# First loads in order of use, one weight block converted earlier, and the first pairs' squared ReLU on another engine

## The reference

```python
h = rmsnorm(x, norm_mix[0]); z = h @ w_in                       # 1024 -> 2304
xa, gc, gb, q, k, v = split(z)
ya = gb * conv3(gc * xa)                                        # causal, width 3
yb = windowed_attention(rmsnorm(q), rmsnorm(k), v, sinks)       # window 128
x = x + concat([ya, yb]) @ w_out
x = x + square(relu(rmsnorm(x, norm_mlp[0]) @ w_up[0])) @ w_down[0]     # 1024 -> 4096 -> 1024
h = rmsnorm(x, norm_mix[1]); x = x + pool_mix(h) * scale        # trailing means of 2, 4, 8, 16
x = x + square(relu(rmsnorm(x, norm_mlp[1]) @ w_up[1])) @ w_down[1]
```

## Time and profile before

| | |
|---|---|
| median of 3 runs | 1857.74 us (1857.17 to 1860.59) |
| the profiled execution | 1856.85 us |
| its span | 1855.1 us |
| PE busy, of the span | 1794.6 us (97%) |
| DVE, ACT, POOL busy | 1286.3, 698.8, 97.2 us |

### The profile page before, as it was taken

How to read it: one execution, slowest core, us unless ns; L and a number is a source line. 1 busy time by engine, 2 the same in 40 slices (tenths; PEclk the granted TensorE clock), 3 DMA queues, 4 the chain that set the end, 5 groups by cost and what they waited for, 6 DMA issues and landing times.

```text
span 1855.1 us, 33339 instructions
## 1 busy us (share of the span) xinstructions
PE 1794.6 (97%) x13805; PEld 1752.4 (94%) x13805; DVE 1286.3 (69%) x1992; ACT 698.8 (38%) x1169; POOL 97.2 (5%) x127
## 2 busy tenths in 40 slices
PE   6999999997999999999999999799999999999999
PEld 5998888997999999999999999699999999999999
DVE  4447775469766666878586766787667677868684
ACT  5433332135333333524243355443333353424331
POOL 1100000140000000000000122100000000000000
PEclk9999999999999999999999999799999999999999
DMA  5311111320443444744445212034434484534432
GB/s 196 107 39 35 35 35 53 97 82 25 166 150 135 154 147 153 272 155 162 149 155 179 80 42 79 20 122 152 167 140 143 156 279 144 186 116 169 158 113 95
DMA packets 154519, 233.75 MB, mean 126 GB/s; under 512 B 6800, under 2 KB 103360, under 8 KB 150624
## 3 DMA queue, kind: packets, MB, share of 16 engines
q1 hardware_dynamic: 150880, 222.31, 34.7%
q0 software_dynamic: 3200, 9.21, 1.7%
q10 hardware_dynamic: 288, 0.09, 0.0%
HBM read 160.40 MB, written 71.47 MB: 125 GB/s over the span
## 4 chain that ended last, share of the span: by engine, by line
PE 79%; DVE 11%; ACT 3%; DMA 3%; issue 2%; SPq 1%; POOL 0%; POOLq 0%; DVEq 0%; ACTq 0%
PE out L783 16%; PE out L785 16%; PE out L784 16%; PE scores L785 4%; PE turned L785 4%; PE scores L784 4%; PE turned L784 4%; PE scores L783 4%; PE turned L783 4%; DVE b_lo L2050 1%; DVE ring L2035 1%; DMA wide<-in_w_down 1%; PE turned L965 1%; DVE b_full L2002 1%; DMA wide<-in_w_up 1%
## 5 line engine op out<-in xcount | busy, mean ns | idle before, releaser
L783 PE MATMUL out<-b_hi,ring 128*128 128x268 f32 (+1 forms) x2048 | 590.2, 288 | 23.5 <-DVE b_lo L2066 7.1
L785 PE MATMUL out<-b_hi,ring 128*128 128x268 f32 (+1 forms) x2048 | 589.7, 288 | 0.0
L784 PE MATMUL out<-b_lo,ring 128*128 128x268 f32 (+1 forms) x2048 | 589.3, 288 | 0.0
L1401 ACT ACTIVATE ring<-wide 128x512 fp32r<-128x512 f32 x384 | 233.1, 627 | 552.3 <-DVE wide L2024 225.9
L783 PEld LDWEIGHTS out<-b_hi,ring 128*128 128x128 f32 x2048 | 390.5, 191 | 26.6 <-DVE ring L2035 13.3
L784 PEld LDWEIGHTS out<-b_lo,ring 128*128 128x128 f32 x2048 | 390.1, 190 | 0.1
L785 PEld LDWEIGHTS out<-b_hi,ring 128*128 128x128 f32 x2048 | 390.2, 191 | 0.0
L2035 DVE TENSOR_TENSOR ring<-wide,ring 128x512 fp32r<-128x512 f32 x384 | 261.8, 690 | 154.2 <-ACT ring L1401 152.9
L783 PE MATMUL out<-act_hi,w_hi 128*128 128x352 f32 (+2 forms) x656 | 219.4, 334 | 10.5 <-DVE act_lo L1750 9.2
L783 PE MATMUL turned<-b_hi,ring 128*128 128x268 f32 (+1 forms) x768 | 219.3, 286 | 3.2 <-ACT rs L1385 3.2
L783 PE MATMUL scores<-b_hi,ring 128*128 128x268 f32 (+1 forms) x768 | 219.1, 285 | 2.0 <-DVE ring L2035 2.0
(11 more groups left out here) (204 smaller groups left out, 2593.9 us busy)
## 6 DMA issues: line engine op xcount, KB each, us to landing
wide<-in_w_up SPq DMA_DIRECT2D x32, 1024.0 KB, 5.8
wide<-in_w_down SPq DMA_DIRECT2D x32, 1024.0 KB, 5.6
b_full<-h_dram SPq DMA_DIRECT2D x28, 1072.0 KB, 5.1
b_full<-h_dram SPq DMA_DIRECT2D x28, 1056.0 KB, 5.4
h_dram<-hid SPq DMA_DIRECT2D x64, 268.0 KB, 2.1
h_dram<-hid SPq DMA_DIRECT2D x64, 264.0 KB, 2.2
h_dram<-hid SPq DMA_DIRECT2D x16, 804.0 KB, 3.7
h_dram<-hid SPq DMA_DIRECT2D x16, 792.0 KB, 3.5
```

Source lines behind the costliest of these rows:

```text
L783: nc.tensor.matmul(out, lhs[0], rhs[0], start=first, stop=False, skip_group_check=skip)
L784: nc.tensor.matmul(out, lhs[0], rhs[1], start=False, stop=False, skip_group_check=skip)
L785: return nc.tensor.matmul(out, lhs[1], rhs[0], start=False, stop=last, skip_group_check=skip)
L1401: nc.scalar.activation(cells(ring, n, 0), left_source(U, q), ACT.Copy).then_inc(left_hi, 1)
```

## The change

- **w_in packed.** The host lays the 18 blocks of w_in out as `w_in_units` (18, 128, 8, 128), so that a partition's share of a block is one run of 4 KB instead of eight of 512 B.
- **SP's order.** Blocks 0, 1 and 2 are now issued before x of pieces 1 and 2. Block 2 waits for `split_lo(0)`, and the eight x DMAs stand behind that wait.
- **POOL's order.** The DMAs of the masks and what follows them in POOL's queue (conv state, three copies of old state) wait until x of piece 2 is in.
- **Input projection.** `norm_hi` and `act_ready` count single chunks. ACT and DVE do blocks 1 and 2 ahead of the norm's parts in another order, and pieces 1 and 2 of the activations earlier or later (below). PE does `norm_stats(0)` after unit 1 instead of unit 0.
- **MLP 1, end of w_out.** `scale_chunk` on ACT also covers piece 2, `normed(1, 2, .)` becomes one multiplication, `first_rights(0, 2, T1)` moves behind the last `add_output`, and the two `first_right` parts of piece 1 move one step ahead.
- **First pairs.** The ReLU and the square of `hidden11` and `hidden22` of units 0, 1, 32 and 33 go from one DVE instruction to two ACT instructions (`hidden_square`). DVE keeps the addition.
- **MLP 2.** `left_hi_part(33, A12)` on ACT moves ahead of `squares(2, 4, 8)`. On DVE `sums(32)` moves ahead of `left_lo_part(33, A12)`.

```diff
@@ SP
             load_in(1)
+            load_in(2)
             load_x(1)
             load_x(2)
-            for w in range(2, W_OUT):
+            for w in range(3, W_OUT):
                 load_in(w)
@@ POOL
+            for i in range(4):
+                pool.wait_ge(x_in[2][i], 16)
             pool.dma_start(const[:, C_MASK:C_COLS], ...).then_inc(masks_in, 16)
@@ PE
-                    if normed_k is not None and k % 2 == 0:
-                        pe.wait_ge(act_ready, 4 * normed_k + k // 2 + 1)
+                    if normed_k is not None:
+                        pe.wait_ge(act_ready, 8 * normed_k + k + 1)
...
-                if m == 0:
+                if m == 1:
                     pe.wait_ge(ident_in, 16)
                     pe.wait_ge(mean_in, 16)
                     norm_stats(0)
@@ ACT, input projection (DVE alike)
+            split_hi(1)
             norm_square(0, 0)
-            split_hi(1)
             norm_square(0, 1)
+            split_hi(2)
+            for pair in range(4):
+                norm_split_hi(1, pair)
             act.wait_ge(eps_ready, 1)
             norm_rsqrt(0)
-            split_hi(2)
...
-                if m in (0, 3):
+                if m == 2:
                     for pair in range(4):
-                        norm_split_hi(p + 1, pair)
+                        norm_split_hi(2, pair)
@@ ACT
+            def hidden_square(U, d, read, made):
+                act.wait_ge(acc_read[read], U + 1)
+                dst = hid_view(d, U)
+                nc.scalar.activation(dst, dst, ACT.Relu).then_inc(act_step, 1)
+                act_steps[0] += 1
+                act.wait_ge(act_step, act_steps[0])
+                nc.scalar.activation(dst, dst, ACT.Square).then_inc(made[U % 2], 1)
@@ ACT, first_pair
                 left_hi_part(b, S3)
+                hidden_square(a, 0, 1, h11_made)
+                hidden_square(b, 0, 1, h11_made)
                 first_right_hi(B22, a)
...
                 left_hi_part(b, A22)
+                hidden_square(a, 2, 4, h22_made)
+                hidden_square(b, 2, 4, h22_made)
@@ ACT, tile 9 of the pooling mixer
                     first_right_hi(B21, UNITS, 1)
+                    left_hi_part(UNITS + 1, A12)
                     squares(2, 4, 8)
@@ DVE, normed
-                if p == 3:
+                if p == 3 or n == 1 and p == 2:
@@ DVE, hidden11 and hidden22
+                if U % UNITS < 2:
+                    return
@@ DVE, first_pair
                 if L:
+                    sums(a)
                     left_lo_part(b, A12)
-                    sums(a)
...
                 else:
+                    first_rights(a, 2, T1)
                     normed(n, 2, 1)
@@ DVE, last piece of w_out
                         if oc == 5:
                             normed(1, 2, 0)
-                        if oc == 6:
-                            first_rights(0, 2, T1)
```

More of the change, by code:

```diff
@@ L1534, in first_pair @@
                 if L:
-                    left_hi_part(b, A12)
                     rsqrt(n, 2)
@@ L1761, in _ @@
                 norm_split_lo(0, pair)
+            split_lo(1)
             norm_reduce(0, 0)
-            split_lo(1)
             norm_reduce(0, 1)
+            split_lo(2)
+            for pair in range(4):
+                norm_split_lo(1, pair)
             dve.wait_ge(norm_rs_done, 1)
-            split_lo(2)
             heads = [m for m in range(18) if m >= 9 or m % 3 != 1]
@@ L1806, in _ @@
                     finish(m - 2)
[L1807 removed]
+                if m == 2:
                     for pair in range(4):
[L1809 removed]
+                        norm_split_lo(2, pair)
                 if m in (1, 4):
```

59 lines of the change are left out of this document (31 added, 28 removed).

## The result

The changed kernel ran in 1840.76 us (median of 4 runs, 1838.69 to 1841.28) beside 1858.7 us for the kernel before (4 runs, 1857.17 to 1860.59). The ratio is 0.9899, with a 95% interval of 0.9886 to 0.9911: faster by 1.0%. Applied to the 1857.74 us of the forecast it gives 1839.0 us, where I had said 1844.2 and 1840.5 to 1850.5. The profiled execution took 1840.58 us with a span of 1838.8, so its span is 16.3 us shorter than before. I had said 13.5. The direction and the places were right; three terms had the wrong size.

What follows compares the result with a forecast made beforehand. PE, busy 1794.6 of 1855.1 us, was taken as the bound, with gains only where it waits. Start 7.2, MLP 1 4.3 and MLP 2 2.0 summed to 13.5 us, forecasting 1844.2 us, range 1840.5 to 1850.5.

Steps and rivals of the forecast that it cites:

- Start, 7.2 forecast: Input projection: 8.2 us won at piece 1's statistics, less 1.65 for bank 1, plus 0.6 for a norm-sum wait.
- my walk from block 1 on: Input projection: instruction times added up from block 1 landing at 12.8 to PE's statistics of piece 1 at 32.35.
- the head-statistics wait: Input projection, behind unit 2: PE waits 1.1 us for DVE's eight `act_lo` of piece 1 and a square.
- the wait for bank 1: Input projection: PE wants bank 1 (v) at 37.8 but it is freed at 39.4, 1.65 us lost.
- MLP 1, 4.3 forecast: Start of MLP 1 to behind unit 2: 2.6 us earlier plus 1.7 us of slow stretch gone; low 1.3, high 5.
- The first product: Start of MLP 1: PE's first product waits 3.1 us instead of 4.59, net 1.5 us won.
- the clock is likely to fall in the wait as before: MLP 1's first product: the clock falls in the wait, so PE's statistics gain no more than about 1.35 us.
- The slow stretch behind unit 2: MLP 1: PE's wait shrinks from 1.99 to about 1.0 us, so the slow clock behind it goes, 1.7 us.
- MLP 2, 2.0 forecast: Start of MLP 2: first product's shift of 0.64 + 0.2 plus PE's wait of 1.19 us; 0.9 to 3.2.
- The bounds are 0.5 (POOL first each time) and 2.3 (POOL behind all three): Start of MLP 2: limits in us on the delay of POOL's additions with DVE's three sums beside them.
- My most likely case, turns: Start of MLP 2: DVE's three sums take turns with POOL, 1.7 us of delay, `normed` 0.2 us earlier.
- The one on interference: Rival: POOL and DVE do not get in each other's way; start 8.2, MLP 2 3.2, 1842 us; chance 0.10.

Runs made afterwards that it cites:

- the kernel without the squares: Changed kernel with ReLU and square of units 0, 1, 32 and 33 back on DVE, one instruction each: 1845.28 us, ratio 0.9922.
- the start alone: Kernel before with all changes of the input projection and no others: 1849.68 us, ratio 0.9946.
- SP's order: Changed kernel with block 2 again issued behind x of pieces 1 and 2: 1843.16 us, ratio 0.9909; its profiled execution took 1942.33 us.
- moves undone: Changed kernel with ACT's A12 conversion of unit 33 and DVE's sums of unit 32 back in their old places before MLP 2: 1841.56 us, ratio 0.9901.
- DVE's additions: Changed kernel with DVE instead of POOL adding nine squares before MLP 2, and bank 1 freed earlier in the input projection: 1835.94 us, ratio 0.9871.
- POOL's wait out: Changed kernel without POOL's wait for x of piece 2, so masks, conv state and copies are issued at once: 1845.92 us, ratio 0.9923.
- packing undone: Changed kernel with w_in laid out as before, all orders as changed: 1839.67 us, ratio 0.9895.
- the changed kernel's second profile: The changed kernel run once more, unaltered: 1838.58 us, ratio 0.9893.

## Why the prediction was right where it was, and wrong

The whole gain came out 3 to 5 us larger than forecast (16.3 us by the two profiles, 18.8 by the ratio). Two terms were too small: MLP 1 by 2.7 us, where two steps failed, and the start by 2.3, where only sizes were off. MLP 2 was 1.0 us too large, for one step that failed.

- **Start, 7.2 forecast, 9.5 measured.** The mechanism held: block 1's high part starts at 12.25 (12 to 13.5 forecast), unit 0 ends at 13.9 as forecast, the first statistics are at 19.31 (20.1), the second at 31.00 (32.35). The mis-sized terms all stand in my walk from block 1 on: I let block 1 land at 12.8 and added each instruction's full length, 6.1 us for the norm and then block 2's low part to 21.2; block 2's low part was done at 20.3. That made the head-statistics wait 0.49 instead of 1.1 and the wait for bank 1 1.00 instead of 1.65. The sentence "Packed blocks are otherwise worth nothing" is wrong for the first matmul (1.0 to 1.6 us) and not refuted for unit 7. I gave the reason for block 1's 15.1 us as x and POOL's copies together. The runs show 2.1 us for the copies alone and none for x alone, which delays block 2 by 2.9 us; for both together they show nothing.
- **MLP 1, 4.3 forecast, 7.0 measured.** Two steps failed. The first product: 0.94 and 1.26 us came as said, but I then took 0.65 us off for ACT's later A11. DVE's part of it comes 0.6 us earlier instead (412.15 against 420.73, with 8.0 us of shift), since the parts of B11 and B21 stand one step ahead. So 2.85 instead of 1.5. And "the clock is likely to fall in the wait as before": after 1.74 us it did not, which gave 1.3 us more. The squares came to 1.65 (1.9 forecast), and their ReLUs were covered.
- **The slow stretch behind unit 2.** It went, as forecast, and with it 1.5 us, but that was luck. The reason I gave, the length of the wait, is refuted by the kernel without the squares (2.08 us and a clock of 1.00), and the start alone, with the old MLP 1, has no slow stretch there either. What decides it stays open.
- **MLP 2, 2.0 forecast, 1.0 measured.** The squares gave 1.9 to 2.5. The step that failed is "The bounds are 0.5 (POOL first each time) and 2.3 (POOL behind all three)": the addition was held up by 3.1 us, since it also waited for the low part ahead of the sums and the ring part behind them, which I had not counted as members of the row. My most likely case, turns (additions over 1.2 us near 1170; the longest is 1.18 to 1.53), is what four of seven profiles show; the one I forecast for showed the other. The Trainium skill ("SBUF — State Buffer", section "Who interferes with whom") has the two engines exclude each other for a whole instruction, by issue order. By that rule the turns agree. The addition of 3.95 us does not: its record begins at 1152.87, ahead of the first sum at 1153.63, and it still ended behind that sum and the three instructions after it.
- **Not in the forecast at all:** the clock's fall at 300 us (-1.5), and +0.7 and -0.4 us in waits far behind the change.
- **The rivals.** None came. PEclk was at 1.00 from unit 1 to unit 7 (24 matmuls in 4.1 to 4.3 us), block 1 was not late, the squares did leave the path. The one on interference had the opposite sign in the profile that was taken. The measured median of 1840.76 lies just inside my range, the 1839.0 us that the ratio gives 1.5 us below it. Its lower end took the start as good to 8.5 and MLP 1 to 5, and these were 9.5 and 7.0; with MLP 2 at 3.2 these terms give 1841.0, so the 1840.5 lies 0.5 us under its own sum.

## What to carry to other kernels

At a start, what is not needed at once should wait for what is, on every queue: the copies in another engine's queue cost 2.1 us and the order in the same queue 2.9, while packing showed nothing sure beyond the first matmul. A POOL instruction that a chain depends on should not stand beside a row of DVE instructions with two operands from memory; where DVE idles, it can do the work itself or wait. A wait that is shortened can give back its length and the slow clock behind it, so price both; and before an effect of 1 or 2 us is put down to an edit, look at the same stretch in two or three profiles of the same code, and at the granted clock in each.

## What the runs showed of the hardware that was not expected

- The granted clock falls while PE is busy without a break. The windows at 300 to 308 or 312 to 320 us show 0.57 to 0.95 with PE busy 4.00 of 4.00 us in nine of the twelve profiles of changed kernels (SP's order is left out): at one of the two places in six, at both in three (moves undone, DVE's additions, POOL's wait out). There is none in the other three (start alone, packing undone, the changed kernel's second profile) and none in the kernel before. One fall costs about 1.5 us. No edit goes with it.
- POOL's addition beside a row of DVE instructions has two outcomes with the same code, 3.95 to 3.97 us for one of them or 1.18 to 1.53 for the longest, and which it is moves unit 34 by 1.5 us. The long one came in the three profiles whose clock was 1.00 from 12 to 14 us behind the mixer's first statistics, the turns in the four where it was 0.50.
- After waits of 0.94 to 2.08 us ahead of unit 2 in MLP 1 the clock stayed at 1.00 in every profile but that of the kernel before (1.99 us, 0.59).
